# Two more pairs of chunks in a seven-product form: the second output projection of a two-block network

## The chip, the cores and the metric

The kernel runs on one core of one Trainium2 chip. The metric is the device time of one launch in microseconds (us), median of several runs.

## What is computed

Two network blocks on 256 tokens of width 2048, all in float32. The first block has two layers: a gated MLP with spatial mixing, and a stick-breaking attention. The part that matters here is the end of the attention layer:

```python
proj = xn @ w_in                        # q, k, v, zg: 2048 columns each
o = stick_breaking_attention(q, k, v)
o = o.reshape(B, S, SB_WIDTH) * jax.nn.silu(zg)
return o @ w_out                        # b_w_out, 2048 x 2048
# h = h + y, then rms_norm(h, final_g), then the second block's rmsnorm and x @ w_in_2
```

The second block (a chunked recurrent branch beside a block attention, and a feed-forward layer of width 8192) follows in the same launch.

## The kernel before

**Tiling.** Every large product is cut into chunks of 512 output columns. `plan` (L83) lists the chunks in the order in which they are computed; for the stretch in question these are `zg` 0 to 3 (the gate, 2048 columns of `b_w_in`), `b_out` 0 to 3 (the second output projection), then `mq` 0, `gates` and `mk` 0 of the second block. A chunk of depth 2048 has 8 groups; a group is one weight tile of 2 x 128 rows x 512 columns (512 KB). Precision comes from splitting both operands into a high and a low part, and each product of a 128x128 token tile with a 128x512 weight tile is three matmuls: high by low, high by high, low by high (`three`, L2425). There are two halves of 128 tokens, so a plain group is 2 x 2 x 3 = 12 matmuls.

**The engines.** Each engine has its own program, written out by hand, and semaphores order them.
- SP (`sync`, L526) issues the weight loads and the DMAs that carry transposed quadrants between partitions. `slot(n)` (L538) first issues every load that is due by group n + 3, then `send` (L541) waits for the DVE's transposes of a chunk and issues four slices of 128 KB.
- ACT (`scalar`, L712) makes the high part of each weight tile (`highs`, L726). `slot(n)` there means: high parts up to group n + 3. A high part of group j waits for its load and for the matmuls of group j - 5 (`N_SPLIT` = 5 buffers).
- DVE (`vector`, L1298) makes the low part (`lows`, L1310) under the same rule, and most of the element work.
- PE (`tensor`, L2421) runs the groups in order (`products`, L2437). It waits for the low part of each.
- Pool issues the small row loads (`load_row`, L677): the rows of `final_g` for chunks 2 and 3 are loaded when chunks 0 and 1 have used theirs.

**Pairs in seven products.** `halved_pairs` (L127) names pairs of chunks for which the first 4 of the 16 depth tiles (k 0 to 3) are multiplied as a 2 x 2 block product in seven products instead of eight: P1, P5, P6, P7 first, then P2, P3, P4. Each product is 6 matmuls. Four operand differences of the weights are made on DVE (`operand`, L1315; L1322 to L1332), sums of the tokens once for all pairs that share them (`split_sums` L1432, `sum_low` L1439, `sum_high` L767), and the results of P1, P5, P6, P7 are put together by `apart` (ACT, L773) and `together` (DVE, L1446). `groups_of` (L251) gives the order of a pair's own groups: a4, P2, b4, P3, a6, P4, b6, a8, b8, a10, b10, a12, a14, b12, b14, where a and b are the two chunks and the number is the first of the group's two k tiles. P1, P5, P6 and P7 stand between the last four groups of whatever comes before. In the kernel before, the first block's `a_out` has one such pair for each half of its depth, and the `up` and `down` chunks of the feed-forward layer run as pairs back to back; `b_out` is plain.

**The work behind each `b_out` chunk** before the change: DVE adds the result to `hres` (`hb`), transposes it in 32x32 blocks, multiplies `hres` by the row of `final_g` (`final`), ACT squares `hres` before and after this, SP sends the transposes, ACT and DVE make the high and low parts of the gained tokens for `mq` 0 (`gained_highs` L757, `gained_lows` L1362). Behind chunk 3 the DVE makes the two norms (`h12`, L1776), which ACT needs to evacuate `mq` 0.

Of the kernel before, what the change touches and what calls it, by code (L numbers as in the profile page):

```python
# [15 lines left out]
D = 2048  # L16
# [110 lines left out]
def halved_pairs():  # L127

    return ([(("v", c), ("v", c + 1)) for c in (4, 6)] +
            [(("a_out", h, 2), ("a_out", h, 3)) for h in range(2)] +  # L130
            [(("gm", c), ("ga", c)) for c in (2, 3)] +
            [(("w_out", 0), ("w_out", 1))] +
            [((kind, q, c), (kind, q, c + 1)) for q in range(4) for kind in ("up", "down") for c in (0, 2)
             if (kind, q) != ("up", 0) and (kind, q, c) != ("down", 3, 2)])
# [7 lines left out]
def _program(nc, A, out, ctx):  # L142
    at = [((nc.sbuf_base + 511) // 512) * 512]

    def sb(name, shape, dt=F32, offset=None):
        size = int(np.prod(shape[1:])) * (2 if dt == BF16 else 4)
        where = at[0] if offset is None else offset
        if offset is None:
# [32 lines left out]
    mth, _ = sb("mth", [128, 16, S], F32R, offset=v_at)  # L181
    mtl, _ = sb("mtl", [128, 16, S], F32R, offset=v_at + 16384)

    vtile = (vreg[:, 1024:2048].rearrange("p (a b) -> p a b", a=2), vreg[:, 5120:6144].rearrange("p (a b) -> p a b", a=2))
    stage = [stage_[:, i] for i in range(N_STAGE)] + [ubuf[:, 0], ubuf[:, 1], spare[:, 0], spare[:, 1], pool4[:, 3], rowb,
                                                      vtile[0], vtile[1]]
    gc, _ = sb("gc", [128, 112])
    cw, _ = sb("cw", [128, 64])
    cosb, _ = sb("cosb", [128, 2, 64])
# [115 lines left out]
    loads_, source, last_of = [], {}, {}  # L305
    opens = {("up", 0, 0): [(N_STAGE + i, N_STAGE, lambda: used.at(where[first_of["w_out", 0], P3])) for i in range(N_MORE)]}
    closes = {}
    for h in range(2):
        opens["a_out", h, 1] = [(s, 2, lambda h=h: prod.at("mix", 4 * h + 3, 1)) for s in (11, 12)]
        closes["a_out", h, 2] = (11, 12)  # L310
# [48 lines left out]
    def sums_of(m):  # L359

        name = pairs[m][0]
        if name[0] == "v":
            return ("v",), yth[:, 0:4, :], yth[:, 4:8, :], mo[:, 0, 1024:2048]
        if name[0] == "a_out":
            return ("y", name[1]), mth[:, 0:4, :], mtl[:, 0:4, :], vreg[:, 4096:5120]
        if name[0] == "gm":
            return ("x2",), us[:, 0:4, :], us[:, 4:8, :], uraw[:, 1]
        if name[0] == "w_out":
            return ("mt",), us[:, 0:4, :], us[:, 4:8, :], uraw[:, 1]
        if name[0] == "up":  # L370
            return ("x3",), rsum, mtl[:, 12:16, :], vreg[:, 7168:8192]
        return ("up", name[1]), sum_h, sum_l, sum_raw

    def quarters(m):

        kind = pairs[m][0][0]
        if kind == "v":
            return [spare[:, 2 + n // 2, n % 2] for n in range(4)]
        if kind in ("gm", "up", "a_out"):
# [332 lines left out]
    def scalar(e):  # L712
# [16 lines left out]
        def slot(n):  # L729
            highs(n + 3)  # L730
# [236 lines left out]
        zg_high(0)  # L967
        zg_high(1)
        zg_gate(2)
        zg_high(2)  # L970
        zg_gate(3)
        zg_high(3)

        for c in range(4):
            slot(end("b_out", c) + 2)
            e.wait_ge(*vec.at("hb", c))
            for i in range(2):
                squares(hres[:, i, cols(c)], ssq[:, i, c:c + 1], "hb", c, i)
            for i in range(2):
                e.wait_ge(*vec.at("final", c, i))  # L980
                squares(hres[:, i, cols(c)], ssq2[:, i, c:c + 1], "final", c, i)
            slot(end("b_out", c) + (5 if c == 3 else 4))
            gained_highs(c, gmix, "x2", c)


        def conv_pad(name, c, b):
# [311 lines left out]
    def vector(e):  # L1298
# [432 lines left out]
        zg_low(0)  # L1731
        zg_turn(1)
        zg_low(1)
        zg_gate(2)
        zg_turn(2)
        zg_low(2)
        zg_gate(3)
        zg_turn(3)
        zg_low(3)

        for c in range(4):
# [5 lines left out]
            if c == 3:  # L1747
                e.wait_ge(*vec.at("hb", 3))
                e.memset(pad[:, :, 0:3], 0.0).then_inc(*vec("pad0"))
            slot(end("b_out", c) + 1)  # L1750
            e.wait_ge(*vec.at("hb", c))
            turn_chunk(lambda i: hres[:, i, cols(c)], flat[zt_buf[c]], "x2", c)
            slot(end("b_out", c) + 2)
# [6 lines left out]
            if c == 3:  # L1760
                both = rq[:, 1, 0:4]
                v12, v1 = both[:, 0:2], both[:, 2:4]
                eps1 = rq[:, 0, 4:6]
                e.tensor_reduce(v1, ssq[:, :, 0:4], AX, ALU.add).then_inc(*vec())
                after_own()
                e.tensor_scalar(v1, v1, 1.0 / D, EPS, ALU.mult, ALU.add).then_inc(*vec())
                after_own()
                e.tensor_scalar(eps1, v1, EPS, None, ALU.mult).then_inc(*vec())
                e.wait_ge(*square.at("final", 3, 1))
                e.tensor_reduce(v12, ssq2[:, :, 0:4], AX, ALU.add).then_inc(*vec())  # L1770
                after_own()
                e.scalar_tensor_tensor(out=v12, in0=v12, scalar=1.0 / D, in1=eps1, op0=ALU.mult,
                                       op1=ALU.add).then_inc(*vec())
                rsqrt(s12_1, both, 4)
                after_own()
                e.tensor_scalar(h12, s12, 0.5, None, ALU.mult).then_inc(*vec("h12"))  # L1776
            slot(end("b_out", c) + (5 if c == 3 else 4))
            gained_lows(c, gmix, "x2", c)


        slot(when(428))
# [639 lines left out]
    def tensor(e):  # L2421
# [49 lines left out]
        def halved(m, f, j):  # L2471

            a, b = pairs[m]
            bank = {P1: banks[4], P5: banks[5], P6: banks[6], P7: banks[7], P2: accs(*a)[0], P3: accs(*b)[0],
                    P4: accs(*a)[1]}[f]
            if f <= P7:
                bank_of(4 + f)
                free[4 + f] = (act.at("first", m), vec.at("w", "pair", m), vec.at("u2", m), vec.at("u3", m))[f]
            key, sum_h, sum_l, _ = sums_of(m)
            xh, xl, t0 = stationary(a)  # L2480
            if f in (P1, P2) and a[0] == "down":
                e.wait_ge(*arrival(("down", a[1], 0), 0))
            elif f in (P1, P2) and a[0] == "w_out":
                e.wait_ge(*arrival(("w_out", 0), 0))
            elif f == P5:
                e.wait_ge(*xlo.at("sums", *key))
            for n in range(2):
                h, l = {P1: (tokens(xh, t0 + 2 * n, 0), tokens(xl, t0 + 2 * n, 0)),
                        P2: (tokens(xh, t0 + 2 * n + 1, 0), tokens(xl, t0 + 2 * n + 1, 0)),
                        P4: (tokens(xh, t0 + 2 * n + 1, 1), tokens(xl, t0 + 2 * n + 1, 1)),  # L2490
                        P5: (tokens(sum_h, 0, n), tokens(sum_l, 0, n)),
                        P6: (tokens(sum_h, 1, n), tokens(sum_l, 1, n)),
                        P7: (tokens(sum_h, 2, n), tokens(sum_l, 2, n)),
                        P3: (tokens(sum_h, 3, n), tokens(sum_l, 3, n))}[f]
# [366 lines left out]
```

## Time and profile before

| | us |
|---|---|
| median of 3 runs | 2550.94 (2549.61 to 2550.96) |
| profiled execution | 2550.57, its span 2548.6 |
| TensorE (PE) busy | 2542.5 |
| VectorE (DVE) busy | 1865.1 |
| ScalarE (ACT) busy | 1323.7 |
| loads of weights | 512 KB each, 4.2 to 5.3 us from issue to landing (medians by tensor) |

A busy engine is one that has an instruction under way; matmuls overlap, so PE's busy time doesn't say how dense its stream is. The granted clock of PE is that which the throttle gave, as a share of full speed; it is 1.00 throughout. In a timeline a row gives the start, the time it took, the engine, the line, the operation, output and inputs, and how many instructions it merges; in brackets the idle time before it, and what ended that.

### The profile page before, as it was taken

Reading aid. Unit: us, or ns where it says so; the run is one execution under the profiler, and the core shown is the slowest. Engines: PE = TensorE matmul, PEld = TensorE weight load, DVE = VectorE, ACT = ScalarE, POOL = GpSimd, SP = SyncE. Lnnn points to the kernel's source line nnn. Section 1 sums busy time; section 2 is a strip of 40 time slices with the busy share of each in tenths; the row PEclk is TensorE's granted clock in tenths of the full one; section 3 lists DMA queues with packets and bytes.
Section 4 is the critical chain, followed back from the end, with each engine's and each line's share of the span. In section 5 each row is a group of like instructions: output and inputs, shape, how many; then the busy total and the mean of one; then the engine's idle time right before and its main releaser. Section 6 shows DMA issues by size and latency. Waiting matters only on the chain.

```text
span 2548.6 us, 29599 instructions
## 1 busy us (share of the span) xinstructions
PE 2542.5 (100%) x11383; PEld 2107.5 (83%) x11383; DVE 1865.1 (73%) x2181; ACT 1323.7 (52%) x1585; POOL 34.9 (1%) x56
## 2 busy tenths in 40 slices
PE   9999999999999999999999999999999999999999
PEld 7888888888888888888888888888888888888887
DVE  6866567566866666776866876778678789899796
ACT  6654444444555555455444544445565456465563
POOL 1000000000000000000000000000020000000000
PEclk9999999999999999999999999999999999999999
DMA  8766776676787777778566787666757676667674
GB/s 282 210 204 197 210 208 193 196 207 198 209 225 201 216 195 205 219 217 231 165 183 181 206 225 198 205 206 198 241 171 230 191 212 209 218 201 230 195 229 157
DMA packets 534796, 527.43 MB, mean 207 GB/s; under 512 B 294896, under 2 KB 297824, under 8 KB 534656
## 3 DMA queue, kind: packets, MB, share of 16 engines
q1 hardware_dynamic: 531856, 518.09, 68.4%
q0 software_dynamic: 2384, 6.93, 1.1%
q8 instruction: 90, 1.47, 0.2%
q10 hardware_dynamic: 416, 0.52, 0.1%
q14 instruction: 50, 0.41, 0.0%
HBM read 488.24 MB, written 2.10 MB: 192 GB/s over the span
## 4 chain that ended last, share of the span: by engine, by line
PE 97%; DVE 2%; SPq 0%; DMA 0%; ACT 0%; issue 0%; DVEq 0%
PE bank L2429 29%; PE bank L2431 29%; PE bank L2430 29%; PE bank L2496 2%; PE bank L2498 2%; PE bank L2497 2%; DVE t_wl L1310 1%; PE bank L2615 1%; PE bank L2604 1%; PE bank L2594 1%; SPq L548 0%; DMA t_stage<-in_a_w_in_dram 0%; PE bank L2537 0%; PE bank L2550 0%; PE bank L2543 0%; DVE t_ytl L1359 0%
## 5 line engine op out<-in xcount | busy, mean ns | idle before, releaser
L1310 DVE TENSOR_TENSOR t_wl<-t_stage,t_wh 128x1024 fp32r<-128x1024 f32 x837 | 1012.1, 1221 | 479.8 <-ACT t_wh L726 472.8
L726 ACT ACTIVATE t_wh<-t_stage 128x1024 fp32r<-128x1024 f32 x838 | 878.0, 1057 | 753.5 <-PE bank L2431 696.9
L2429 PE MATMUL bank<-t_wl,t_xth 128*128 128x512 f32 x2320 | 909.9, 392 | 0.4 <-DVE t_xtl L1352 0.4
L2431 PE MATMUL bank<-t_wh,t_xtl 128*128 128x512 f32 x2320 | 903.0, 389 | 0.0
L2430 PE MATMUL bank<-t_wh,t_xth 128*128 128x512 f32 x2320 | 902.8, 389 | 0.0
L2431 PEld LDWEIGHTS bank<-t_wh,t_xtl 128*128 128x128 f32 x2320 | 435.5, 188 | 90.9
L2429 PEld LDWEIGHTS bank<-t_wl,t_xth 128*128 128x128 f32 x2320 | 435.6, 188 | 90.4 <-DVE t_xtl L1352 0.9
L2430 PEld LDWEIGHTS bank<-t_wh,t_xth 128*128 128x128 f32 x2320 | 435.7, 188 | 89.6 <-issue 0.2
L2429 PE MATMUL bank<-t_wl,t_yth 128*128 128x512 f32 x882 | 343.4, 389 | 0.1
L2430 PE MATMUL bank<-t_wh,t_yth 128*128 128x512 f32 x882 | 342.7, 389 | 0.0
L2431 PE MATMUL bank<-t_wh,t_ytl 128*128 128x512 f32 x882 | 342.7, 389 | 0.0
L2429 PEld LDWEIGHTS bank<-t_wl,t_yth 128*128 128x128 f32 x882 | 165.6, 188 | 34.7 <-DVE t_wl L1310 0.8
L2431 PEld LDWEIGHTS bank<-t_wh,t_ytl 128*128 128x128 f32 x882 | 165.6, 188 | 34.4
L2430 PEld LDWEIGHTS bank<-t_wh,t_yth 128*128 128x128 f32 x882 | 165.6, 188 | 34.1
L726 ACT ACTIVATE t_wh<-t_ubuf 128x1024 fp32r<-128x1024 f32 x91 | 95.5, 1056 | 77.0 <-PE bank L2431 55.9
L1310 DVE TENSOR_TENSOR t_wl<-t_ubuf,t_wh 128x1024 fp32r<-128x1024 f32 x91 | 110.5, 1221 | 33.6 <-ACT t_wh L726 32.6
L1371 DVE STREAM_TRANSPOSE t_pool<-t_pool 128x512 f32<-128x512 f32 x96 | 99.5, 1076 | 0.0
L754 ACT ACTIVATE t_yth<-t_ytl 128x1024 fp32r<-128x1024 f32 x32 | 33.8, 1057 | 46.6 <-DMA t_ytl<-t_pool 46.1
L1359 DVE SCALAR_TENSOR_TENSOR t_ytl<-t_ytl,t_yth 128x1024 fp32r<-128x1024 f32 x32 | 39.2, 1224 | 21.6 <-ACT t_yth L754 21.5
L2498 PE MATMUL bank<-t_wh,t_mtl 128*128 128x512 f32 x126 | 49.0, 389 | 0.0
L2429 PE MATMUL bank<-t_wl,t_mth 128*128 128x512 f32 x112 | 43.7, 390 | 0.0
L2431 PE MATMUL bank<-t_wh,t_mtl 128*128 128x512 f32 x112 | 43.6, 389 | 0.0
(441 smaller groups left out, 1810.3 us busy)
## 6 DMA issues: line engine op xcount, KB each, us to landing
t_stage<-in_a_w_in_dram SPq DMA_DIRECT2D x182, 512.0 KB, 4.4
t_stage<-in_w_in_dram SPq DMA_DIRECT2D x168, 512.0 KB, 4.2
t_stage<-in_b_w_in_dram SPq DMA_DIRECT2D x128, 512.0 KB, 4.4
t_stage<-in_w_down_dram SPq DMA_DIRECT2D x92, 512.0 KB, 5.3
t_stage<-in_w_up_dram SPq DMA_DIRECT2D x91, 512.0 KB, 4.5
t_stage<-in_a_w_out_dram SPq DMA_DIRECT2D x60, 512.0 KB, 4.4
t_ubuf<-in_w_up_dram SPq DMA_DIRECT2D x37, 512.0 KB, 4.6
t_ubuf<-in_w_down_dram SPq DMA_DIRECT2D x36, 512.0 KB, 5.3
```

The source lines that it names most:

```text
L726: e.activation(wh[:, j % N_SPLIT], stage[s], ACT.Copy).then_inc(*hi(j))
L754: e.activation(xh[:, 4 * c:4 * c + 4, :], xl[:, 4 * c:4 * c + 4, :].bitcast(F32), ACT.Copy, scale=scale).then_inc(*xhi(*name))
L1310: e.tensor_tensor(low, src, high.bitcast(F32), ALU.subtract).then_inc(*lo(j))
L1359: e.scalar_tensor_tensor(out=low, in0=low.bitcast(F32), scalar=scale, in1=high.bitcast(F32), op0=ALU.mult, op1=ALU.subtract).then_inc(*xlo ...
L1371: e.transpose(turn_out(dst, i), turn_in(src(i))).then_inc(*turned(*name) if i else turned())
L2429: e.matmul(o, h, w_l, start=start, stop=False)
L2430: e.matmul(o, h, w_h, start=False, stop=False)
L2431: return e.matmul(o, l, w_h, start=False, stop=stop)
L2496: e.matmul(bank, h, w_l, start=n == 0 and f <= P7, stop=False)
L2497: e.matmul(bank, h, w_h, start=False, stop=False)
L2498: last = e.matmul(bank, l, w_h, start=False, stop=n == 1 and f <= P7)
L2594: last = e.matmul(t[:, part], wst[:, 2 * c + j, :], v_tile(c, i)[:, part], start=True, stop=True)
```

## The change

The four chunks of `b_out` become two pairs, (0, 1) and (2, 3). Each pair's seven products use the tokens of k 0 to 3, which are the output of gating chunk 0; their sums are made on DVE and ACT around the end of gating chunk 2. The first product tiles of the first pair are loaded into two further tiles (`vtile[2]`, `vtile[3]`), which are free from the end of the last attention weighting. The products P1, P5, P6, P7 of pair (0, 1) are put between the last groups of `zg` 3, those of pair (2, 3) between the last groups of pair (0, 1).

The epilogues are reordered. DVE now adds the pairs' results into `hres` (`to_result`), sums chunks 0 and 1 behind chunk 1's end, and only then transposes both; the rows of `final_g` for chunks 0 and 1 come after the gained lows of chunk 1, those of chunks 2 and 3 after the gained lows of chunk 3, with the norms behind them. ACT makes the gained highs of chunks 0 and 1 together. SP's program keeps its text: `slot(end("b_out", c) + 1)`, then the send.

```diff
+            [(("b_out", c), ("b_out", c + 1)) for c in (0, 2)] +
...
+    opens["zg", 3] = [(s, 2, lambda: prod.at("weigh", 3, 2)) for s in (13, 14)]
+    closes["b_out", 2] = (13, 14)
...
@@ scalar @@
+        slot(end("zg", 2) + 1)
+        sum_high("zg")
         zg_high(2)
+        apart(first_of["b_out", 0], turned.at("zg", 2))
         zg_gate(3)
         zg_high(3)
...
+        apart(first_of["b_out", 2], vec.at("early", first_of["b_out", 0], 1))
+        hb_squares(0)
+        hb_squares(1)
+        slot(end("b_out", 1) + 4)
+        gained_highs(0, gmix, "x2", 0)
+        gained_highs(1, gmix, "x2", 1)
+        slot(end("b_out", 1) + 8)
+        final_squares(0)
+        final_squares(1)
+        hb_squares(2)
+        hb_squares(3)
+        for c in (2, 3):
+            slot(end("b_out", 3) + (2, 5)[c - 2])
             gained_highs(c, gmix, "x2", c)
+        final_squares(2)
+        final_squares(3)
...
@@ vector @@
+        slot(end("zg", 2) - 3)
+        e.wait_ge(*prod.at("weigh", 3, 2))
+        split_sums(yth, ytl, vreg[:, 4096:5120], vreg[:, 5120:6144], "zg")
         zg_gate(2)
+        slot(end("zg", 2) + 2)
+        sum_low("zg")
...
+        def to_result(m):
+
+            e.wait_ge(*vec.at("w", "pair", m))
+            for n in range(2):
+                d = hres[:, :, cols(pairs[m][n][1])]
+                e.tensor_tensor(d, d, buf[n], ALU.add).then_inc(*vec("early", m, n))
+                e.wait_ge(*vec.at("early", m, n))
+
+        m = first_of["b_out", 0]
+        together(m, turned.at("zg", 3))
+        slot(where[m, P4] + 1)
+        to_result(m)
+        out_sum(0)
+        out_sum(1)
+        out_turn(0)
+        out_turn(1)
+        m = first_of["b_out", 2]
+        slot(end("b_out", 1) + 4)
+        gained_lows(0, gmix, "x2", 0)
+        together(m, vec.at("early", first_of["b_out", 0], 1))
+        slot(end("b_out", 1) + 6)
+        gained_lows(1, gmix, "x2", 1)
+        final_row(0)
+        final_row(1)
+        to_result(m)
+        out_sum(2)
+        out_turn(2)
+        out_sum(3)
+        e.wait_ge(*vec.at("hb", 3))
+        e.memset(pad[:, :, 0:3], 0.0).then_inc(*vec("pad0"))
+        out_turn(3)
+        slot(end("b_out", 3) + 2)
+        gained_lows(2, gmix, "x2", 2)
+        slot(end("b_out", 3) + 5)
+        gained_lows(3, gmix, "x2", 3)
+        final_row(2)
+        final_row(3)
...
@@ tensor @@
+            elif f in (P1, P2) and a == ("b_out", 0):
+                e.wait_ge(*arrival(a, 0))
```

## Rows read from the trace of the kernel before

**Rows 1.** The page: busy time by engine; the chain that ended last, by engine.
```profile
PE 2542.5 (100%) x11383; PEld 2107.5 (83%) x11383; DVE 1865.1 (73%) x2181; ACT 1323.7 (52%) x1585; POOL 34.9 (1%) x56
...
PE 97%; DVE 2%; SPq 0%; DMA 0%; ACT 0%; issue 0%; DVEq 0%
```

**Rows 2.** The waits of PE, longest first: total, times, longest one (us).
```profile
PE bank L2555 <- DVE t_pool L1464: 1.2, 1, 1.2
```

**Rows 3.** Timeline of PE in the fourth output chunk, nine matmuls on end.
```profile
1159.63 0.39 PE L2429 MATMUL bank<-t_wl,t_yth 128*128 128x512 f32 x1
...
1161.44 0.39 PE L2431 MATMUL bank<-t_wh,t_ytl 128*128 128x512 f32 x1
```

**Rows 4.** Timeline of DVE behind output chunks 0 and 2.
```profile
1106.79 1.28 DVE L1746 TENSOR_TENSOR t_hres<-t_hres,bank 128x512 f32<-128x512 f32 x2 [0.34 <-PE bank L2431]
...
1109.12 2.09 DVE L1371 STREAM_TRANSPOSE t_pool<-t_hres 128x512 f32<-128x512 f32 x2
1111.13 1.19 DVE L1310 TENSOR_TENSOR t_wl<-t_stage,t_wh 128x1024 fp32r<-128x1024 f32 x1
1112.23 1.29 DVE L1759 TENSOR_TENSOR t_hres<-t_hres,t_rowb 128x512 f32<-128x512 f32 x2
...
1161.29 1.67 DVE L1365 SCALAR_TENSOR_TENSOR t_xtl<-t_xtl,t_gmix,t_xth 128x256 fp32r<-128x256 f32 x4
1162.88 1.22 DVE L1310 TENSOR_TENSOR t_wl<-t_stage,t_wh 128x1024 fp32r<-128x1024 f32 x1
```

**Rows 5.** Timeline of DVE in the feed-forward stage, where pairs follow each other.
```profile
2096.40 0.68 DVE L1459 TENSOR_TENSOR t_pool<-bank,t_pool 128x512 f32<-128x512 f32 x1
2097.00 0.68 DVE L1461 TENSOR_TENSOR t_pool<-bank,t_pool 128x512 f32<-128x512 f32 x1
...
2109.91 1.22 DVE L1310 TENSOR_TENSOR t_wl<-t_stage,t_wh 128x1024 fp32r<-128x1024 f32 x1
2111.05 1.22 DVE L1329 TENSOR_TENSOR t_ubuf<-t_stage,t_ubuf 128x1024 f32<-128x1024 f32 x1
```

**Rows 6.** Windows: length, busy us (instructions) by engine, granted clock, DMA share, GB/s.
```profile
1063.27:1172.07 108.80, 108.80 (x481) 90.12 (x480) 77.11 (x85) 58.57 (x82) 1.08 (x2) 1.00 0.78 225
2540.00:2548.60 8.60, 4.47 (x20) 2.66 (x19) 4.96 (x14) 2.31 (x7) 0.00 (x0) 1.00 0.47 179
```

**Rows 7.** Timeline of ACT: a gate's start, and the gained highs of chunks 0, 1, 2.
```profile
1063.27 1.27 ACT L956 ACTIVATE t_pool<-bank,t_scl 128x512 f32<-128x512 f32 x2 [1.60 <-PE bank L2431]
...
1118.45 1.71 ACT L761 ACTIVATE t_xth<-t_xtl,t_gmix 128x256 fp32r<-128x256 f32 x4 [2.06 <-DMA t_xtl<-t_pool]
...
1141.79 1.71 ACT L761 ACTIVATE t_xth<-t_xtl,t_gmix 128x256 fp32r<-128x256 f32 x4 [3.64 <-DMA t_xtl<-t_pool]
...
1160.18 1.71 ACT L761 ACTIVATE t_xth<-t_xtl,t_gmix 128x256 fp32r<-128x256 f32 x4 [0.26 <-DMA t_xtl<-t_pool]
```

**Rows 8.** Timeline of SP's queue: two loads on end; the sends behind chunks 0, 1, 2.
```profile
717.88 1.43 SPq L535 DMA_DIRECT2D t_stage<-in_b_w_in_dram  x2
...
1111.24 3.35 SPq L548 DMA_DIRECT2D t_xtl<-t_pool  x4
...
1133.00 2.99 SPq L548 DMA_DIRECT2D t_xtl<-t_pool  x4
...
1154.77 3.05 SPq L548 DMA_DIRECT2D t_xtl<-t_pool  x4
```

**Rows 9.** DMA issues right behind those sends (1114.6, 1136.0, 1157.9): KB, us to landing.
```profile
t_stage<-in_b_w_out_dram SPq DMA_DIRECT2D x1, 512.0 KB, 5.5
...
t_stage<-in_b_w_out_dram SPq DMA_DIRECT2D x1, 512.0 KB, 7.0
...
t_stage<-in_w_in_dram SPq DMA_DIRECT2D x1, 512.0 KB, 4.4
```

**Rows 10.** Timeline of DVE behind chunk 3: first and last operation of the norms.
```profile
1178.85 0.14 DVE L1764 TENSOR_REDUCE t_rq<-t_ssq 128x2 f32<-128x8 f32 x1
...
1182.49 0.17 DVE L1776 TENSOR_SCALAR t_scl<-t_scl 128x2 f32<-128x2 f32 x1
```

More of the change, by code:

```diff
@@ L182, in _program @@
     mtl, _ = sb("mtl", [128, 16, S], F32R, offset=v_at + 16384)
-    vtile = (vreg[:, 1024:2048].rearrange("p (a b) -> p a b", a=2), vreg[:, 5120:6144].rearrange("p (a b) -> p a b", a=2))
+    vtile = [vreg[:, n:n + 1024].rearrange("p (a b) -> p a b", a=2) for n in (1024, 5120, 6144, 7168)]
     stage = [stage_[:, i] for i in range(N_STAGE)] + [ubuf[:, 0], ubuf[:, 1], spare[:, 0], spare[:, 1], pool4[:, 3], rowb,
-                                                      vtile[0], vtile[1]]
+                                                      vtile[0], vtile[1], vtile[2], vtile[3]]
     gc, _ = sb("gc", [128, 112])
@@ L365, in sums_of @@
             return ("y", name[1]), mth[:, 0:4, :], mtl[:, 0:4, :], vreg[:, 4096:5120]
+        if name[0] == "b_out":
+            return ("zg",), mtl[:, 0:4, :], mtl[:, 4:8, :], vreg[:, 5120:6144]
         if name[0] == "gm":
@@ L378, in quarters @@
             return [spare[:, 2 + n // 2, n % 2] for n in range(4)]
-        if kind in ("gm", "up", "a_out"):
+        if kind in ("gm", "up", "a_out", "b_out"):
             return [buf[n // 2][:, n % 2, :] for n in range(4)]
@@ L969, in scalar, with hb_squares @@
         zg_gate(2)
+        slot(end("zg", 2) + 1)
+        sum_high("zg")
         zg_high(2)
+        apart(first_of["b_out", 0], turned.at("zg", 2))
         zg_gate(3)
         zg_high(3)
-        for c in range(4):
+        def hb_squares(c):
             slot(end("b_out", c) + 2)
@@ L978, in scalar, with final_squares @@
                 squares(hres[:, i, cols(c)], ssq[:, i, c:c + 1], "hb", c, i)
+        def final_squares(c):
             for i in range(2):
@@ L981, in scalar @@
                 squares(hres[:, i, cols(c)], ssq2[:, i, c:c + 1], "final", c, i)
-            slot(end("b_out", c) + (5 if c == 3 else 4))
+        apart(first_of["b_out", 2], vec.at("early", first_of["b_out", 0], 1))
[11 more added lines that the diff above has]
+            slot(end("b_out", 3) + (2, 5)[c - 2])
             gained_highs(c, gmix, "x2", c)
+        final_squares(2)
+        final_squares(3)
         def conv_pad(name, c, b):
@@ L1739, in vector, with out_sum @@
         zg_low(3)
-        for c in range(4):
+        def out_sum(c):
             slot(end("b_out", c))
@@ L1746, in vector, with out_turn @@
                 e.tensor_tensor(hr, hr, accs("b_out", c)[i], ALU.add).then_inc(*vec("hb", c) if i else vec())
-            if c == 3:
-                e.wait_ge(*vec.at("hb", 3))
-                e.memset(pad[:, :, 0:3], 0.0).then_inc(*vec("pad0"))
+        def out_turn(c):
             slot(end("b_out", c) + 1)
@@ L1752, in vector, with final_row @@
             turn_chunk(lambda i: hres[:, i, cols(c)], flat[zt_buf[c]], "x2", c)
+        def final_row(c):
             slot(end("b_out", c) + 2)
@@ L1759, in vector @@
                 e.tensor_tensor(hr, hr, rowb[:, c % 2, :], ALU.mult).then_inc(*vec("final", c, i))
[L1760 to L1776, printed above, removed]
@@ L1777, in vector @@
-            slot(end("b_out", c) + (5 if c == 3 else 4))
-            gained_lows(c, gmix, "x2", c)
+        def to_result(m):
[7 more added lines that the diff above has]
+        slot(where[m, P4] + 1)
@@ new lines, in vector @@
+        e.memset(pad[:, :, 0:3], 0.0).then_inc(*vec("pad0"))
[6 more added lines that the diff above has]
+        final_row(3)
+        both = rq[:, 1, 0:4]
+        v12, v1 = both[:, 0:2], both[:, 2:4]
+        eps1 = rq[:, 0, 4:6]
+        e.tensor_reduce(v1, ssq[:, :, 0:4], AX, ALU.add).then_inc(*vec())
+        after_own()
+        e.tensor_scalar(v1, v1, 1.0 / D, EPS, ALU.mult, ALU.add).then_inc(*vec())
@@ new lines, in vector @@
+        after_own()
+        e.tensor_scalar(eps1, v1, EPS, None, ALU.mult).then_inc(*vec())
+        e.wait_ge(*square.at("final", 3, 1))
+        e.tensor_reduce(v12, ssq2[:, :, 0:4], AX, ALU.add).then_inc(*vec())
+        after_own()
+        e.scalar_tensor_tensor(out=v12, in0=v12, scalar=1.0 / D, in1=eps1, op0=ALU.mult,
+                               op1=ALU.add).then_inc(*vec())
+        rsqrt(s12_1, both, 4)
+        after_own()
+        e.tensor_scalar(h12, s12, 0.5, None, ALU.mult).then_inc(*vec("h12"))
```

## The prediction

> **What bounds the kernel now.** I read the page first: TensorE (PE) is busy for the whole span, VectorE (DVE) for 73% of it, and the chain that ended last runs through PE for 97% [rows 1]. Then the waits: the longest of PE in the whole run is 1.2 us [rows 2], and its line is run only in the first microseconds. So a matmul that is taken away shortens the run by its place in the stream, and a wait that is added lengthens it. Next, the price of a matmul: a row says 0.39 us, but this counts the pipeline's depth. The starts are what matters: from 1159.63 to 1161.44 us there are eight steps, 0.226 us each [rows 3]. The timelines of DVE, ScalarE (ACT) and the load queue (SP) tell the rest. From ACT's gate of the third gating chunk at 1063.27 to DVE's sum of the first chunk of the second output projection at 1106.79 are 16 groups in 43.52 us [rows 4, 7]: a group of 12 matmuls takes 2.72 us, and PE never stands there.
>
> **What is taken away.** A pair of chunks has 192 matmuls of this shape. The paired form gives 7 products of 6 for 4 plain groups of 12, so 42 for 48. Two pairs save 12 matmuls, 12 x 0.2267 = 2.72 us. This is certain to leave the stream, as nothing covers it. If nothing else moved, the profiled execution would go from 2550.57 us (span 2548.6 and 2.0 around it) to 2547.85. The median of the runs shown is 2550.94, 0.4 above that execution; the sum below is made against 2550.57. What a measurement can tell from no change is 0.2%, 5.1 us, so even the whole saving would be within it.
>
> The trace's step can be set against the Trainium skill. The page "TensorE: Matmul & The Clock Gate", section "Back-to-back issue gap", gives about 131 ns for each matmul of 512 columns in a sustained stream with weight loads, and 216 ns for one by the other formula. By the first the saving would be 1.6 us, by the second 2.6; the rows here speak for the second.
>
> **What is added and does not show at first.** Each pair adds 3 weight tiles to split (7 for 4): ACT 1.06 and DVE 1.14 us each, four operand differences of 1.14 us, four sums of PSUM results of 0.60 us, and two additions of 128x1024 into the result of 1.14 us, with DVE's steps from start to start of these shapes [rows 5]. For both pairs DVE gets 6 x 1.14 + 8 x 1.14 + 8 x 0.60 + 4 x 1.14 = 25.3 us, and 5 to 6 us more for the operand sums in the third gating chunk (one 128x1024 addition, four of 128x256, one low part), half of it ahead of the stretch. From the start of the fourth gating chunk to the end of the projection DVE is busy for 77 of 108.8 us [rows 6]. Some 3 us (chunk 2's gained lows and gain row) leave the stretch, so about 102 us of work come to 106: DVE becomes nearly as full as PE. The feed-forward stage runs pairs back to back, with DVE as dense as in rows 5, and no PE wait there is among the longest. So it can hold, but without slack. The sums in the third gating chunk I cost at nothing: due some 8 groups before their use, they are hidden by the split tiles made ahead; without that cover they cost their 5 to 6 us. What decides is the order: engines work in order, and a tile is split at most 5 groups ahead. I lay out the one place where the new order bunches the work, behind chunk 1.
>
> **The place behind chunk 1, step by step.** PE's order after chunk 1 is A4 (chunk 2, k 4), product, B4 (chunk 3), product, A6, product, B6, A8, B8, A10, B10. The third gating chunk ends at 1063.27 on ACT's row [rows 7]. From there 8 groups and 4 products (27.2 us), then 12 groups and 7 products (42.16) end chunk 1; DVE's out_sum(1) starts at X = 1132.63. PE, 0.37 us ahead of that row, reaches B10 after 7 groups and 3 products, at 1132.26 + 23.12 = 1155.38, if it never waits.
>
> 1. SP. At end(chunk 0) + 1 it waits for the transposes of chunk 0. Before, they followed chunk 0's sum. Now the DVE does both sums first, after chunk 1, 8.2 us later. out_sum(1) takes 1.20 and the two transposes 2.01 [rows 4]: they are done at 1135.84. Behind this wait in SP's queue stand the weight loads from A8's on. SP sends 4 slices (3.0 to 3.4 us [rows 8]), so A8's load is issued at 1139.1. A load right behind such a send lands after 5.5 us, in the rows 4.4 to 7.0 [rows 9]: 1144.6 (1143.5 to 1146.1). Then ACT's high part (1.06) and the start of DVE's low part: 1145.7 (1144.6 to 1147.2).
> 2. SP issues four loads (0.7 each [rows 8]) and sends chunk 1's transpose from 1141.9 on. From a send's first slice to the ACT work that waits for it: 1111.24 to 1118.45 is 7.2 us, 1133.00 to 1141.79 is 8.8, 1154.77 to 1160.18 is 5.4 [rows 7, 8]. I take the middle, 7.2: 1149.1 (1147.3 to 1150.7). ACT must make both chunks' gained highs before B8's high part: 4 x 0.405 and 1.06, so B8's low part starts no sooner than 1151.8 (1150.0 to 1153.4).
> 3. DVE by its own queue: A8's low part, 4 gained lows of chunk 0 (1.59 [rows 4]), the four sums of the second pair (2.5 with the pauses between them): 5.25 us, so it is free for B8's low part at 1150.95 (1149.85 to 1152.45). Step 2 ends last.
> 4. Between A10's low part and B10's DVE now has, in its order, chunk 1's gained lows (1.59), the final-gain rows of chunks 0 and 1 (2 x 1.20) and the additions into the result (2 x 1.14): 6.3 us. With B8's, A10's and B10's own low parts (3.4) and the signal (0.1) it is 9.8 us: B10 is ready at 1161.6 (1159.8 to 1163.2).
>
> PE needed it at 1155.4. So PE stops for 6.2 us in all (4.4 to 7.8), some 2 to 3 of them at B8 and 3.4 at B10. Against the 2.72 taken away this makes +3.5 us (+1.7 to +5.1): 2554.1 us.
>
> By the Trainium skill a load would be quicker: "DMA: Bandwidth & Descriptors", section "Anatomy of one DMA — SWDGE (gpsimd) path", fits 2.0 us plus the bytes over 436 GB/s for that path, 3.2 us for a load of this size. It would end step 1 some 2 us sooner and change the sum by nothing, as step 2 ends last.
>
> **The end of the projection.** Chunks 2 and 3 finish as the second pair of the first block's output projection does, which stops PE nowhere; nothing there. The final norm, now behind chunk 3's gained lows, takes 3.8 us of small DVE operations [rows 10]. By the same steps chunk 3's gained lows end 14.6 us behind the end of the projection (4 groups of mq 0, then ACT's and DVE's parts), the gain rows at 17.0, ACT's squares at about 19.5, the norms at 22. ACT wants them at 21.8, when mq 0 ends; the second gates group, whose weight tile waits behind them on DVE, starts at about 23.7. Its cost is nothing to 1 us, and I take nothing.
>
> **Rivals.**
> - Hidden after all (18%). If chunk 1's slices land in 5.4 us, and DVE has done some of its work while PE was busy with A6 and B6, the bunch is eaten by the tiles split ahead, and PE stops for under 3.7 us. The time is then 2547.9 (no stop) to 2551.6. For it speaks that PE waits for none of the existing pairs; against it that 9.8 us of DVE work stand in one piece between B8 and B10, where PE has 5.4 us of work and what is split ahead, and that nothing else may start the load of A8 sooner.
> - Slower by over 0.2% (18%). One mechanism: the landing of chunk 1's transposed slices, on which ACT stands with the high parts of four groups behind it. Every microsecond beyond 7.2 is one of PE's. From 8.8 us on, which one row shows [rows 7, 8], PE stops for 7.8 us and the run is 5.1 us slower; at 12 us it would be 2559. For it: four loads of 512 KB stand ahead of it in the same queue. Against: the row of 8.8 us had a row load of GpSimd beside it, and there is none here.
> - The clock (4%). Half of that stop is in one piece. In the last 8.6 us of the run PE is busy for 4.5 only and the granted clock is 1.00 [rows 6], as in every stretch that I read. Should it fall to 1.2 GHz behind the stop, each microsecond there would lose half of itself, and over 3 us of it would bring the run beyond 2556. The Trainium skill's "TensorE: Matmul & The Clock Gate", section "HAM oscillation — how this bites in real kernels", warns of such gaps between matmuls; no row of this kernel shows a fall.
> - My forecast, +1.1 to +5.1 us: 60%.
>
> **How the numbers follow.** The likeliest is 2554.1. Within 0.2% are the forecast and nearly all of the first rival: 0.77. Slower: the second and third rivals, 0.22; stops at the first pair, where by the same counting DVE leaves PE 2 to 3 us in hand, would add to the same side and are in them. Faster by 5.1 us has no source: 0.01. The range leaves about a tenth out on each side: 2549.8 to 2557.0, from a stop of 2 us to one of 9.
>
> **What would show it.** The profile after should have 12 matmuls fewer, PE waits of L1310's low part at two places some 87 to 99 us behind the start of the fourth gating chunk, 5 to 7 us together; SP waiting about 8 us for chunk 0's transposes; ACT idle behind a slice transfer just before PE's stop; granted clock 1.00. If PE's waits are near nothing, step 4 was wrong; if they are there but elsewhere, step 1 or 2. Were the time under 2549, the bunch would not exist.

## The result, and the profile after

The changed kernel takes 2556.73 us (median of 10 runs, 2555.87 to 2557.58), the kernel before 2550.44 us beside it (2549.61 to 2551.43): a ratio of 1.0024, 95% interval 1.0016 to 1.0032. Twelve matmuls are gone and the run is 6.3 us longer. The profiled executions differ by nearly as much, 2556.16 us (span 2554.4) against 2550.57: +5.6.

The page after, its busy row, answers to the one of before [rows 1]:

```profile
PE 2542.3 (100%) x11371; PEld 2106.7 (82%) x11371; DVE 1894.4 (74%) x2213; ACT 1331.3 (52%) x1594; POOL 34.9 (1%) x56
```

TensorE (PE) has 12 instructions fewer but is busy for the same 2542 us, so the ones left took longer. VectorE (DVE) has 29 us more. The waits of PE, longest first (total, times, longest one), against [rows 2]:

```profile
PE bank L2495 <- DVE t_wl L1335: 6.2, 3, 4.9
PE bank L2623 <- DVE t_pool L1489: 1.2, 1, 1.2
```

Before, the wait at the run's start (1.2) was the longest. Now PE waits 6.2 us in three waits for low parts of weight tiles, made by DVE; the smallest, 0.3 us, is at 2329 us, in the feed-forward stage. The timeline of PE says where the other two are (start, duration, engine, line, operation; in brackets the idle time before it and what ended it). It starts at B8, chunk 3's group of k 8, and ends at B10:

```profile
1155.12 0.80 PE L2495 MATMUL bank<-t_wl,t_yth 128*128 128x512 f32 x1 [4.94 <-DVE t_wl L1335]
1155.71 0.63 PE L2496 MATMUL bank<-t_wh,t_yth 128*128 128x512 f32 x1
...
1159.56 0.44 PE L2496 MATMUL bank<-t_wh,t_yth 128*128 128x512 f32 x1
1159.83 0.40 PE L2497 MATMUL bank<-t_wh,t_ytl 128*128 128x512 f32 x1
1160.07 0.40 PE L2495 MATMUL bank<-t_wl,t_yth 128*128 128x512 f32 x1
...
1163.90 0.50 PE L2495 MATMUL bank<-t_wl,t_yth 128*128 128x512 f32 x1 [0.93 <-DVE t_wl L1335]
```

Two stops: 4.94 us at B8 and 0.93 us at B10. Between them is a third loss that no wait shows. From 1155.71 to 1159.56 the starts are 0.43 us apart, then 0.23, as in [rows 3]. The windows around it (length; then busy us and instructions by engine; then granted clock, DMA share, GB/s) name it:

```profile
1145.00:1150.00 5.00, 5.00 (x23) 3.94 (x21) 4.89 (x9) 1.43 (x4) 0.00 (x0) 1.00 1.07 266
1150.00:1155.00 5.00, 0.18 (x1) 0.00 (x0) 1.42 (x3) 3.84 (x7) 0.00 (x0) 0.78 0.71 219
1155.00:1160.00 5.00, 4.88 (x12) 3.86 (x13) 5.00 (x10) 3.10 (x6) 0.54 (x1) 0.54 0.61 192
1160.00:1165.00 5.00, 4.07 (x18) 3.02 (x18) 4.93 (x6) 4.29 (x7) 0.54 (x1) 1.00 0.39 128
```

The granted clock is 0.54 where the matmuls are at half pace: the level of 1.2 GHz, come during the stop and gone at 1159.6. The ten steps from 1155.12 to 1159.56 took 4.44 us and not 2.27. That is 2.2 us. The fall is not peculiar to this trace: the mean granted clock of all ten executions is 0.998 or 0.999, and 1.000 in the kernel before.

The account of the stretch: 24 matmuls stand between B8's first and B10's first, 5.4 us at full pace. PE stood ready for B8 at 1155.12 - 4.94 = 1150.18, so it would have wanted B10 at 1155.6; it came at 1163.90, 8.3 us late. 8.3 less the 2.7 taken away is the +5.6 of the profiled executions. So all the time is lost in this one stretch.

Whom did B8 wait for? DVE waited for ScalarE (ACT), and ACT for a transfer (timelines of ACT, DVE and the load queue SP in the same stretch; compare [rows 7, 8]):

```profile
1143.77 1.06 ACT L731 ACTIVATE t_wh<-t_stage 128x1024 fp32r<-128x1024 f32 x1 [5.07 <-DMA t_stage<-in_b_w_out_dram]
1144.73 1.69 ACT L766 ACTIVATE t_xth<-t_xtl,t_gmix 128x256 fp32r<-128x256 f32 x4
1151.16 1.70 ACT L766 ACTIVATE t_xth<-t_xtl,t_gmix 128x256 fp32r<-128x256 f32 x4 [4.73 <-DMA t_xtl<-t_pool]
1152.77 3.88 ACT L731 ACTIVATE t_wh<-t_stage 128x1024 fp32r<-128x1024 f32 x4
```

```profile
1153.84 2.36 DVE L1335 TENSOR_TENSOR t_wl<-t_stage,t_wh 128x1024 fp32r<-128x1024 f32 x2 [3.58 <-ACT t_wh L731]
1156.12 1.67 DVE L1390 SCALAR_TENSOR_TENSOR t_xtl<-t_xtl,t_gmix,t_xth 128x256 fp32r<-128x256 f32 x4
1157.70 2.49 DVE L1790 TENSOR_TENSOR t_hres<-t_hres,t_rowb 128x512 f32<-128x512 f32 x4
1160.11 2.48 DVE L1797 TENSOR_TENSOR t_hres<-t_hres,t_pool 128x1024 f32<-128x1024 f32 x2
1162.62 5.76 DVE L1335 TENSOR_TENSOR t_wl<-t_stage,t_wh 128x1024 fp32r<-128x1024 f32 x5
```

```profile
1135.83 3.02 SPq L553 DMA_DIRECT2D t_xtl<-t_pool  x4
1138.89 2.33 SPq L540 DMA_DIRECT2D t_stage<-in_b_w_out_dram  x4
1141.33 7.08 SPq L553 DMA_DIRECT2D t_xtl<-t_pool  x4
```

ACT stands for 4.73 us, waiting for the transposed slices of chunk 1. They are sent from 1141.33 and reach ACT at 1151.16, 9.8 us later. B8's low part starts at 1153.84 and then DVE works without a gap through the low parts of B8 and A10, chunk 1's gained lows, the final-gain rows and the additions, up to B10's low part at 1162.62. The sending itself is odd: four issues take 3.02 us at 1135.83 and 7.08 us at 1141.33. The experiments turn on that row.

### The profile page after: what moved, and what is told of

Read it like the earlier page. It is cut to its first block, busy times and chain, and to the rows that moved or that the text cites. A ratio compares the mean times of both kernels' runs of the same rounds, so it can differ in the third digit from the quotient of the medians.

```text
span 2554.4 us, 29642 instructions
## 1 busy us (share of the span) xinstructions
PE 2542.3 (100%) x11371; PEld 2106.7 (82%) x11371; DVE 1894.4 (74%) x2213; ACT 1331.3 (52%) x1594; POOL 34.9 (1%) x56
## 4 chain that ended last, share of the span: by engine, by line
PE 98%; DVE 1%; SPq 0%; ACT 0%; DMA 0%; issue 0%; DVEq 0%; ACTq 0%
PE bank L2495 29%; PE bank L2497 29%; PE bank L2496 29%; PE bank L2566 3%; PE bank L2565 3%; PE bank L2564 3%; PE bank L2683 1%; PE bank L2672 1%; PE bank L2662 1%; DVE t_wl L1335 0%; SPq L553 0%; PE bank L2596 0%; PE bank L2605 0%; DVE t_pool L1396 0%; PE bank L2611 0%; PE bank L2618 0%
## 5 line engine op out<-in xcount | busy, mean ns | idle before, releaser
L2495 PE MATMUL bank<-t_wl,t_yth 128*128 128x512 f32 x850 | 332.1, 391 | 6.2 <-DVE t_wl L1335 6.2
L2496 PE MATMUL bank<-t_wh,t_yth 128*128 128x512 f32 x850 | 331.0, 389 | 0.0
L2497 PE MATMUL bank<-t_wh,t_ytl 128*128 128x512 f32 x850 | 331.0, 389 | 0.0
L2495 PEld LDWEIGHTS bank<-t_wl,t_yth 128*128 128x128 f32 x850 | 160.1, 188 | 40.5 <-DVE t_wl L1335 7.5
L2496 PEld LDWEIGHTS bank<-t_wh,t_yth 128*128 128x128 f32 x850 | 160.1, 188 | 33.1
L2497 PEld LDWEIGHTS bank<-t_wh,t_ytl 128*128 128x128 f32 x850 | 160.0, 188 | 33.2
L2566 PE MATMUL bank<-t_wh,t_mtl 128*128 128x512 f32 x142 | 55.2, 389 | 0.0
L2497 PE MATMUL bank<-t_wh,t_mtl 128*128 128x512 f32 x112 | 43.6, 389 | 0.0
```

What stands on the lines that cost most here:

```text
L2495: e.matmul(o, h, w_l, start=start, stop=False)
L2496: e.matmul(o, h, w_h, start=False, stop=False)
L2497: return e.matmul(o, l, w_h, start=False, stop=stop)
```

## The experiments

Theory 1: two delays in a row set the end. The slices of chunk 1 come late because their send stands behind chunk 0's send and four loads, and behind their arrival 9.8 us of VectorE work stand ahead of B10. Rivals: the late load of A8 (ACT's 5.07 us wait) is the cause; or the clock is, with its 2.2 us; or the final-gain rows are what fills VectorE. The same kernel before was run beside each group of kernels (2550.74, 2550.81 and 2550.95 us); the ratios are to those.

### Three loads ahead of the wait

```diff
         for c in range(4):
-            slot(end("b_out", c) + 1)
+            slot(end("b_out", 1) if c == 0 else end("b_out", c) + 1)
             send(flat[zt_buf[c]], quadrants(xtl, c), "x2", c)
```

> The changed kernel, but SP issues three more weight loads (those of A8, B8 and A10) before it waits for chunk 0's transposes. Theory 1 (the order in SP's queue makes chunk 1's slices land late, after 9.8 us instead of 7.2, and ACT stands with the high parts behind them): the slices go out at about 1139 instead of 1141.3 with one load ahead of them instead of four and land after 5.4 to 7.2 us; B8's low part then starts at 1148 to 1150 instead of 1153.8, PE's waits fall from 6.2 us to 2.5 to 4.5, the clock stays at 1.00, and the time is 2550 to 2552. Theory 2 (the four pieces of DVE work between A10 and B10 are the cause by themselves): B10 is still late, PE waits as long as before but at B10, and the time stays within 1 us of 2556. Theory 3 (the clock's fall is the cause of what was not forecast): as the first, since the fall goes with the long stop.

Measured: 2554.52 us (2553.7 to 2558.65), ratio 1.0017 (1.0008 to 1.0026). The profiled execution is the slowest of them, 2558.65; 11 matmuls fewer lie in its first 25 us than in the changed kernel's, so everything in it is some 2 us late before this stage begins (its send of chunk 0 starts at 1138.02, the changed kernel's at 1135.83). ACT, then SP issue by issue around chunk 1's send:

```profile
1151.51 1.71 ACT L766 ACTIVATE t_xth<-t_xtl,t_gmix 128x256 fp32r<-128x256 f32 x4 [6.17 <-DMA t_xtl<-t_pool]
```

```profile
1143.53 3.14 SPq L553 DMA_DIRECT2D t_xtl<-t_pool  x1
1146.72 0.67 SPq L553 DMA_DIRECT2D t_xtl<-t_pool  x1
```

The load of A8 is out of the way: ACT makes A8's high part at 1141.58 and no longer waits for it. Still the slices, sent from 1142.14, are there only at 1151.51, 9.4 us later. So the load of A8 is worth at most the 2.2 us by which this run is below the changed kernel (2.5 against the kernel before beside each). The time is 2.5 us above what I expected at most: I had put the long landing down to the four loads, and it stayed with one. The single issues show a thing that I had not looked at. The third slice is held in SP's queue for 3.14 us, where a slice otherwise takes 0.7, and the fourth can only follow it. PE stops 3.10 us at B8 and 3.04 at B10, with half pace for 8 matmuls behind the second. The median is 4.1 us below this execution, of which the late start explains 2.2, so its landing of 9.4 us need not be that of the others.

### The gained parts of chunk 1 later

```diff
-        gained_highs(1, gmix, "x2", 1)
         slot(end("b_out", 1) + 8)
+        gained_highs(1, gmix, "x2", 1)
```
and on VectorE
```diff
-        gained_lows(1, gmix, "x2", 1)
         ...
+        slot(end("b_out", 1) + 8)
+        gained_lows(1, gmix, "x2", 1)
```

> The changed kernel, with ACT's gained highs of chunk 1 moved behind the high parts of B8 to B10, and DVE's gained lows of chunk 1 moved behind the additions of the second pair; SP as in the changed kernel. Theory 1: ACT no longer stands before B8's high part, whatever the slices take; A8's load is still late (landing at about 1143.7), so PE waits 1 to 2 us at B8 and about 2 at B10, 3.4 us together, no fall of the clock, time 2551 to 2552. Theory 2 (DVE's bunch): DVE's work before B10 is less by the 1.6 us of the gained lows only, so the time falls by under 2 us, to 2554.5 or more.

Measured: 2551.81 us (2550.55 to 2552.69), ratio 1.0004 (0.9995 to 1.0014); profiled 2551.01. PE's stops:

```profile
1152.13 0.50 PE L2496 MATMUL bank<-t_wl,t_yth 128*128 128x512 f32 x1 [1.67 <-DVE t_wl L1335]
1159.33 0.50 PE L2496 MATMUL bank<-t_wl,t_yth 128*128 128x512 f32 x1 [1.43 <-DVE t_wl L1335]
```

As expected: the slices are sent as late as in the changed kernel (issue 1141.80, 7.50 us long), but no weight tile stands behind them, and 4.9 us are won back. 3.1 us of stops less 2.7 is +0.4, the profiled difference. The edit also takes the gained lows, 1.6 us, off VectorE's queue ahead of B10, and ACT's part was not moved alone; but 1.6 us is all that they can be worth, and 4.9 were won. This carries theory 1: the wait that costs is ACT's for the slices, by what is queued behind it.

### Both

The two edits above in one kernel, run twice, 11 times each.

> Both edits together: three loads ahead of SP's wait, and chunk 1's gained highs and lows later. Theory 1: no wait of PE is left in the projection, the clock stays at 1.00, and the saving of 12 matmuls, 2.72 us, shows whole: 2.5 to 3 us faster than the kernel before, 2547.5 to 2548.2. Theory 2: DVE, busy for nearly all of the stretch, still leaves a stop of 2 to 4 us before B10: 2550 or more.

> The same kernel as the one with both edits (three loads ahead of chunk 0's send; the gained parts of chunk 1 behind the next two loads' high parts and behind the attention chunks' sums), a second time and with more rounds, because its first interval (0.9983 to 1.0001) just reached no change. If the saving of twelve matmuls (2.7 us) shows but for the 0.4 us of new waits that its trace has in this stretch, the kernel is 2.3 us below the one before: a ratio of 0.9991. In the trace the third slice of chunk 1's send is again held back (2.2 us in the first trace, 4.8 in the changed kernel) and nothing waits for it. If the gain was chance, the ratio is 1.0000 or above.

Measured: 2548.44 us (2547.36 to 2549.82), ratio 0.9992 (0.9983 to 1.0001); the second time 2548.49 us (2547.01 to 2549.34), ratio 0.9989 (0.9980 to 0.9998). PE's waits of the second, all of them:

```profile
PE bank L2624 <- DVE t_pool L1489: 1.2, 1, 1.2
PE bank L2496 <- DVE t_wl L1335: 0.6, 1, 0.6
PE bank L2496 <- DVE t_xtl L1377: 0.5, 1, 0.5
PE bank L2873 <- ACT t_cpb L1312: 0.4, 1, 0.4
```

None of these is in the stretch: the 0.6 us for a low part are at 2321 us, in the feed-forward stage, as is the 0.4 of that kind in the first trace. Of the change's stops nothing is left. The kernel is 2.3 to 2.5 us below the one before, the twelve matmuls' 2.72 us nearly whole; the first median is 0.2 us above what I expected. So they are worth what the sum said, the whole loss came from the order, and this version beats both kernels, the one before by a tenth of a per cent, which the second interval just shows.

One load still lies between the sends here. In the second trace the second send and the landing of its last slice, issued at 1143.98, are

```profile
1139.91 4.74 SPq L553 DMA_DIRECT2D t_xtl<-t_pool  x4
DMA to landing us min/median/max: 3.3/3.3/3.3
```

so all four slices are there 7.3 us after the first issue, and 6.9 in the first trace. So the 9.4 us in the run with three loads ahead are not simply the price of one load.

### The two sends together

```diff
         for c in range(4):
-            slot(end("b_out", c) + 1)
+            slot(end("b_out", 1) if c < 2 else end("b_out", c) + 1)
             send(flat[zt_buf[c]], quadrants(xtl, c), "x2", c)
```

> Against the changed kernel, SyncE now issues the loads up to B10's but one before the wait for chunk 0's turn, and then both sends, chunk 0's and chunk 1's, with no load between them. It differs from the run that had three loads moved ahead in one point: there one load (B10's) still lay between the two sends, and the slices of chunk 1 were 9.4 us from their issue to the first high part that needs them. Theory 1, from the single issues in that trace: the third slice of the second send is not issued (its issue lasts 3.1 us; 4.8 us in the changed kernel with four loads between) until the load in front has been moved. With nothing between, the four issues take 3 to 4 us and the last slice lands 3.0 us after its own issue: the gained high parts of chunk 1 start 6 to 7.5 us after the send's issue, at 1145 to 1147. Then B8's low part waits for B8's high part at most to 1150 and follows the operand sums, PE stops below 1 us at B8 and, by the 9.8 us of VectorE ahead of B10's low part, for the rest up to 4.5 us in all: 2.7 taken off, +1 to +2 on the kernel before, 2551.5 to 2552.5 us. Theory 2, that two sends close together are slow of themselves: the landing stays at 9 us or more from an issue 3 us sooner (1148), the time is 2553 to 2555. If the landing were worth nothing and the VectorE queue were not the limit, 2548.

Measured: 2551.7 us (2549.36 to 2553.62), ratio 1.0004 (0.9995 to 1.0012). SP and ACT:

```profile
1140.42 3.12 SPq L553 DMA_DIRECT2D t_xtl<-t_pool  x4
```

```profile
1145.95 1.71 ACT L766 ACTIVATE t_xth<-t_xtl,t_gmix 128x256 fp32r<-128x256 f32 x4 [1.46 <-DMA t_xtl<-t_pool]
```

The eight issues run on end from 1136.00; those of chunk 1 are the four shown. Its slices reach ACT 5.5 us after 1140.42: theory 1 said 6 to 7.5, and that two sends are slow because they are close together (9 us) is out. Chunk 0's third slice was held here, for 2.23 us, with its nearest load issued 3.4 us before the send but not yet landed. PE has one stop left in the stretch, 2.91 us at B10 (1158.70), where the 9.8 us of VectorE work alone had to leave one. The clock falls behind it:

```profile
1155.00:1160.00 5.00, 2.09 (x8) 1.40 (x7) 4.93 (x5) 4.15 (x7) 0.54 (x1) 0.91 0.47 138
1160.00:1165.00 5.00, 5.00 (x19) 3.95 (x18) 3.69 (x4) 1.06 (x1) 0.00 (x0) 0.75 0.94 311
```

The profiled execution is 1.7 us above the median. Others were spared the fall: the mean granted clock of the four fastest of the 11 executions (2549.36 to 2551.14 us) is 1.000, that of the seven slower ones 0.999.

### Both sends ahead of the loads

```diff
-            slot(end("b_out", c) + 1)
+            slot(end("b_out", 0) + 1 if c == 1 else end("b_out", c) + 1)
```

> Against the changed kernel, only the four loads (A8, B8, A10, B10) move from between the two sends to behind the second. Theory 1 (the third slice's issue waits until the loads in front of it have been moved): the issues of the second send now take 3 to 4 us and its slices land 6 to 7.5 us after the issue at 1138.9, by 1146.5; but A8's load goes out at 1142.5 to 1143.5 instead of 1138.9 and its high part, 4.4 to 5.5 us later, starts at 1147.5 to 1149, 4 to 5 us later than now. A8's low part, the low parts of chunk 0, the sums, B8's and A10's low parts and the rest of the 9.8 us then run without a gap from 1149 on: PE stops at A8, the first time on this home, 0.5 to 1.5 us, and at B10's low part, ready at 1163.5 to 1165. The time is that of the changed kernel within 1.5 us, 2555.5 to 2558, although the send lands 3 us sooner. Theory 2 (two sends close together are slow of themselves): the second send takes 9 us or more, the high parts of chunk 1 start at 1148 or later, and the time is above 2558.

Measured: 2557.52 us (2557.02 to 2559.32), ratio 1.0028 (1.0017 to 1.0039). The second send's issues take 3.3 us here (1139.38 to 1142.65), for the 7.08 of the changed kernel. But A8's load is 3.8 us later, and ACT and PE show what follows:

```profile
1147.59 1.06 ACT L731 ACTIVATE t_wh<-t_stage 128x1024 fp32r<-128x1024 f32 x1 [8.54 <-DMA t_stage<-in_b_w_out_dram]
1148.55 3.29 ACT L766 ACTIVATE t_xth<-t_xtl,t_gmix 128x256 fp32r<-128x256 f32 x8
```

```profile
1149.95 0.50 PE L2495 MATMUL bank<-t_wl,t_yth 128*128 128x512 f32 x1 [2.15 <-DVE t_wl L1335]
1155.26 0.50 PE L2495 MATMUL bank<-t_wl,t_yth 128*128 128x512 f32 x1 [0.73 <-DVE t_wl L1335]
1164.04 0.50 PE L2495 MATMUL bank<-t_wl,t_yth 128*128 128x512 f32 x1 [3.06 <-DVE t_wl L1335]
```

The stop at A8, 2.15 us, is longer than the 0.5 to 1.5 that I expected. Both chunks' slices are there when ACT comes to them (one row of eight, no wait). The price has only moved: A8, then the same VectorE queue, B10 at 1164.04 for 1163.90. With loads behind the sends A8 is late, with loads between them the slices are. Of the orders tried, the loads ahead of both sends (the run before) or no weight tile queued behind the slices take the price away, each but for stops of about 3 us in all.

### The final rows spread

```diff
+            to_result(m)
+            slot(end("b_out", 1) + 9)
             ...
+            slot(end("b_out", 1) + 11)
             ...
-            to_result(m)
```
(the rows of chunk 0 behind the first new slot, those of chunk 1 behind the second; ACT's squares likewise)

> Against the changed kernel, the rows that end the layer for chunk 0 and chunk 1 (2.5 us of VectorE, with ScalarE's squares behind them) move from ahead of B10's low part to two places behind it. This asks whether VectorE's queue ahead of B10 still sets the end once the slices land late. By the queue, B10's low part is ready 2.5 us sooner, at about 1161.4. The stop at B8 (4.9 us) and the matmuls at half pace behind it stay, so PE comes to B10 at 1163.0 and doesn't wait there any more: 0.9 us gained of the 2.5, and by my sum of the queues 1 to 1.7 us of new stops come behind it, where the moved rows delay the low parts of the gate's first tiles (0.7 to 1.1 each). Theory 1: 2556 to 2557.5, the same as the changed kernel within 1 us, with no wait at B10 and small ones behind it. Rival: the rows find room there and the 0.9 us stays gained or more, 2555 to 2556 or less.

Measured: 2557.98 us (2557.07 to 2558.89), ratio 1.0028 (1.0018 to 1.0039): 0.5 us above the upper end of what I expected. PE stops 5.19 us at B8 and not at B10. Small stops come behind the stretch instead, these two (total, times, longest) and one of 0.2 us:

```profile
PE bank L2498 <- DVE t_xtl L1391: 1.1, 1, 1.1
...
PE bank L2498 <- DVE t_hres L1777: 0.4, 1, 0.4
```

2.5 us taken from VectorE's queue ahead of B10 win only the 0.9 of the stop there, since PE comes late itself, at half pace, and 1.7 come back behind it, as forecast. Another 0.5 us of the profiled difference of 1.8 lies ahead of this stage. So in the changed kernel the rows are not what costs; once the slices are late, room on VectorE is worth nothing.

### The first stop filled with matmuls

```diff
+                    if (name, k0) == (("b_out", 3), 8):
+                        t = bank_of(4)
+                        for _ in range(11):
+                            e.matmul(t[:, 0:256], neg[:, 0:128], mask, start=True, stop=True)
```

> The changed kernel, with 11 matmuls of constants (256 columns in float32, 0.43 us each at the full clock by the rows at the run's end, 4.7 us together) into an idle bank before B8's first matmul, where PE stands for 4.9 us. Nothing of the result uses them. Theory 1 (the end of the stop at B10 is set by DVE's queue, which the clock doesn't touch; the 2 us that ten matmuls lose at half pace are taken from PE's wait at B10, 0.9 us instead of 3.3): the granted clock stays at 1.00, PE's wait at B10 grows from 0.9 to about 3 us, and the time stays within 0.5 us of 2556.7. Theory 3 (the fall of the clock costs its 2 us): the time falls by 2 us.

Measured: 2558.53 us (2557.91 to 2559.53), ratio 1.0032 (1.0020 to 1.0044). PE:

```profile
1150.45 4.91 PE L2528 MATMUL bank<-t_mask,t_neg 128*128 128x256 f32 x22
1155.84 0.50 PE L2495 MATMUL bank<-t_wl,t_yth 128*128 128x512 f32 x1 [0.47 <-DVE t_wl L1335]
...
1164.62 0.50 PE L2495 MATMUL bank<-t_wl,t_yth 128*128 128x512 f32 x1 [3.03 <-DVE t_wl L1335]
...
1166.12 0.63 PE L2495 MATMUL bank<-t_wl,t_yth 128*128 128x512 f32 x1
```

(A float32 matmul of the edit is two instructions in the trace, so 11 are x22.) Kept busy, PE has its full pace behind B8 (starts 0.23 us apart), and the wait at B10 grows from 0.93 to 3.03 us: the 2.2 us of the half pace had been hidden there, as VectorE sets when B10 can start. That half of the theory holds. But the time rose by 1.8 us, where I expected at most 0.5: the clock now fell behind the second stop, at 1166.12, for 8 matmuls, where nothing absorbs it (1.6 us). Of the profiled difference, 2.2 us, another 0.7 lie ahead of this stretch: every operation of it starts that much later. Here the fall ahead of another wait for the same queue was free, and the one behind the last wait was not.

## Why the prediction was right or wrong

The range held the time, and the likeliest number was 2 to 3 us low: +3.5 us was forecast and +5.6 to +6.3 came, outside the +1.1 to +5.1 to which I had given 60%. What came is the second rival: the landing of chunk 1's slices beyond 8.8 us, slower by over 0.2% (+0.24%, at that edge). I had given it 18% and within 0.2% 77%. The place, the order of the steps and which of them ends last were right; one term was too small.

- What is taken away: right. 12 fewer matmuls; with the order mended 2.3 to 2.5 us of the 2.72 show.
- Step 1: right to 1 us. Send at 1135.83 (forecast 1135.84), A8's load at 1138.89 (1139.1), its high part at 1143.77, which is the 1144.6 less 0.8 and ends no wait of PE.
- Step 2: the start of the send was right (1141.33, forecast 1141.9). The term that was mis-sized is the landing: 9.8 us, not 7.2, and beyond my bound of 8.8. Put into the same steps it gives B8's low part at 1153.84 for 1151.8, B10 8.3 to 8.5 us late and +5.6 to +5.8, against +5.6 measured. The three rows from which I took 5.4 to 8.8 [rows 7, 8] had no load straight ahead. In each the loads before the send stop 1.6 us earlier, as these rows of the kernel before show:

```profile
1094.83 14.77 SPq L535 DMA_DIRECT2D t_stage<-in_b_w_out_dram  x8
...
1114.64 16.72 SPq L535 DMA_DIRECT2D t_stage<-in_b_w_out_dram  x8
...
1149.99 3.13 SPq L535 DMA_DIRECT2D t_stage<-in_w_in_dram  x2
```

  (1109.60 to the send at 1111.24, 1131.36 to 1133.00, 1153.12 to 1154.77.) In the changed kernel 0.1 us lie between them. The rival named the right reason, "four loads of 512 KB stand ahead of it in the same queue", and I priced the term by rows in which that reason was absent. The kernel before has rows of a send with loads still under way ahead of it, in the feed-forward stage, and I took the landing from none of them. One has two loads ahead; the second of them and the send are:

```profile
2427.61 0.61 SPq L535 DMA_DIRECT2D t_ubuf<-in_w_up_dram  x1
2429.59 6.58 SPq L548 DMA_DIRECT2D t_ytl<-t_pool  x4
```

  The load lands 8.0 us after its issue, the four slices take 6.58 us to issue, the third alone 4.42, and the last of them lands at 2439.57: 10.0 us from the first issue. With these 10.0 us for the landing the same steps give +6.3 us.
- Step 3: right. VectorE ends the sums at 1150.3 and waits 3.6 us for ACT.
- Step 4: right. 9.8 us from the start of B8's low part to PE's start of B10 was forecast; 1153.84 to 1163.90 is 10.1. The run with the two sends together shows it alone: the slices in time, and still a stop of 2.91 us at B10 (forecast 3.4).
- How the stop is split: wrong, 4.9 and 0.9 for 2 to 3 and 3.4, by the late landing and the clock.
- The clock: I gave this rival 4% and expected a granted clock of 1.00. It fell. Half pace lasted 4.4 us and took 2.2, the half that I had named, but it cost nothing, as the filled stop showed: it came out of the wait at B10.
- Sums in the third gating chunk and the first pair: nothing, as said. No wait of PE lies in 900 to 1100 us. The end of the projection: the norms end at 1199.0, 21.4 us behind it (forecast 22), and PE doesn't wait there.
- "Hidden after all" is ruled out for the changed kernel, and is what the kernel with both edits does.

What stays open: why the landing took 9.4 us in the run with three loads ahead and 6.9 and 7.3 in the two traces with both edits, each with one load between the sends. In the first the load landed after 5.4 us (4.6 and 4.9), and the last slice 4.8 us after its issue (3.2 and 3.3), while the queue's rate was down to 68 GB/s from 1146 to 1148 us. Why the third slice is the one that is held is open too.

## What to carry to other kernels

Price a landing by rows with the same traffic ahead of it in the same queue, if need be from another stage, not by the same transfer elsewhere; read the issues one by one, for a send whose issues take longer than its neighbours' is held, and so is all behind it. When two chunks finish together, their epilogues stand in one piece on every in-order queue: put what the matmuls wait for (weight loads, high parts) ahead of what they don't, on each of the queues; here two such moves turned +6 us into -2.3. Here a stop's clock loss counted only behind the last wait for the same engine.

## What the runs showed of the hardware

- SP's queue holds back the third slice of a send (128 KB each) while a load issued ahead of it has not landed. The single issues of the changed kernel, with four loads of 512 KB just ahead:

```profile
1141.98 0.90 SPq L553 DMA_DIRECT2D t_xtl<-t_pool  x1
1142.93 4.76 SPq L553 DMA_DIRECT2D t_xtl<-t_pool  x1
1147.73 0.67 SPq L553 DMA_DIRECT2D t_xtl<-t_pool  x1
```

- It is let go as the last of those loads lands. In these nine sends the third issue ends 0.04 to 0.16 us before that landing (the load's issue and its time to landing, added):

| send | third issue, us | it ends at | last load ahead lands at |
|---|---|---|---|
| changed kernel, chunk 1 | 4.76 | 1147.69 | 1147.79 |
| three loads ahead, chunk 1 | 3.14 | 1146.67 | 1146.80 |
| gained parts later, chunk 1 | 4.68 | 1148.58 | 1148.64 |
| both edits, chunk 1 | 2.24 | 1143.77 | 1143.84 |
| both edits again, chunk 1 | 2.66 | 1143.93 | 1144.02 |
| sends together, chunk 0 | 2.23 | 1139.61 | 1139.72 |
| rows spread, chunk 1 | 4.48 | 1148.28 | 1148.32 |
| stop filled, chunk 1 | 4.17 | 1148.73 | 1148.89 |
| kernel before, feed-forward stage | 4.42 | 2435.45 | 2435.58 |

  In the ten traces together 86 sends of four slices have a third issue of over 2 us. In 71 of them it ends at most 0.3 us before the landing of the last load ahead; in the others between 0.6 before and 1.2 behind it. Where that load had landed by the end of the third issue, as in the sends of rows 8, the issue took 0.8 to 1.0 us. The last slice can only be issued behind the held one, and in this stretch lands 3.2 to 4.8 us after its own issue. The link is read from these times; no run changed the size of a load or of a slice.
- The granted clock fell to the level of 1.2 GHz behind seven of the stops named here and not behind six. It fell behind 4.94 and 5.19 us (at the first matmul), and behind 2.15, 2.91, 3.03, 3.04 and 3.06 us (0.2 to 1.5 us after the matmuls had begun again). It didn't behind 0.47 (the filled stop), 0.73, 0.93, 1.43 and 1.67 us, nor behind 3.10 us at B8 in the run with three loads ahead. So the length of the stop alone doesn't decide it. Each fall lasted 6 to 10 matmuls, 0.43 us apart for 0.227: 1.2 to 2.2 us.
